# A decoder step: six counts of a sampled search placed behind the units of their pass, and new row blocks in the last norm

## The reference: what is computed

```python
h1 = LN1(alpha*x  + 0.5*SwiGLU_1(x))
h2 = LN2(alpha*h1 + W_out[attn_group(h1) | hgrn2_group(h1)])
y  = LN3(alpha*h2 + 0.5*SwiGLU_2(h2))
...
score = jnp.where(valid, score, -jnp.inf)   # sample tokens: 8192 cached keys and the new one
_, idx = lax.top_k(score, n_sel)            # n_sel = 256
...
xc = x32 - mu
var = jnp.mean(xc * xc, -1, keepdims=True)
return xc * lax.rsqrt(var + LN_EPS) * g + b
```

## Time and profile before

| what | value |
|---|---|
| median of 3 runs | 2416.02 us (2415.59 to 2416.42) |
| profiled execution | 2416.54 us, of which the span of the page is 2414.8 us |
| TensorE busy | 2340.9 us, 97% of the span |
| VectorE, GpSimd, ScalarE busy | 67%, 37%, 30% |
| mean granted clock of TensorE | 0.99 |

### The profile page before, as it was taken

The page is one execution under the profiler, slowest core; times in us unless marked ns, Lnnn a source line. Parts: engine busy times, 40 slices in busy tenths (PEclk is TensorE's granted clock), DMA queues, the critical chain, the costliest instruction groups (busy, mean ns, idle before and its releaser), DMA issues.

```text
span 2414.8 us, 33393 instructions
## 1 busy us (share of the span) xinstructions
PE 2340.9 (97%) x12317; PEld 1926.6 (80%) x12317; DVE 1612.7 (67%) x2577; ACT 714.9 (30%) x1441; POOL 886.7 (37%) x948
## 2 busy tenths in 40 slices
PE   8999999999999999999999899999999999999996
PEld 7888888888887556778777677888888888888885
DVE  6675666578975348897767844236575665678876
ACT  2122222210023246773332356314122222210014
POOL 5354444446475021110000133414244444445570
PEclk9999999999999999999999999999999999999998
DMA  6021222264411033330010112021012131256401
GB/s 184 18 96 53 88 71 70 100 256 148 144 58 35 1 93 114 105 101 20 2 28 2 41 40 69 4 71 35 27 61 80 62 105 53 73 206 243 144 18 71
DMA packets 138047, 192.58 MB, mean 80 GB/s; under 512 B 19112, under 2 KB 86264, under 8 KB 137632
## 3 DMA queue, kind: packets, MB, share of 16 engines
q1 hardware_dynamic: 130096, 169.97, 21.0%
q0 software_dynamic: 7792, 20.48, 3.0%
HBM read 160.10 MB, written 30.06 MB: 79 GB/s over the span
## 4 chain that ended last, share of the span: by engine, by line
PE 88%; DVE 7%; issue 2%; ACT 1%; POOL 1%; DMA 1%; SPq 0%; DVEq 0%; POOLq 0%; ACTq 0%
PE ps L2104 38%; PE ps L2198 16%; PE ps L794 9%; PE ps L799 7%; PE ps L1186 4%; PE ps L1074 2%; PE ps L2201 2%; PE ps L964 2%; PE ps L1048 2%; PE ps L850 1%; PE ps L875 1%; PE ps L1061 1%; PE ps L1014 1%; PE ps L885 1%; PE ps L897 1%
## 5 line engine op out<-in xcount | busy, mean ns | idle before, releaser
L2104 PE MATMUL ps<-big 128*128 128x258 f32 x1760 | 410.5, 381 | 5.1 <-DVE big L2517 4.6
L2104 PEld LDWEIGHTS ps<-big 128*128 128x128 f32 x1760 | 333.0, 190 | 57.1 <-issue 7.7
L2369 ACT ACTIVATE down_weights<-ps 128x258 f32<-128x258 f32 x370 | 142.8, 387 | 699.8 <-PE ps L2104 699.7
L2637 DVE TENSOR_TENSOR down_weights<-ps,down_weights 128x258 f32<-128x258 f32 x330 | 139.3, 425 | 261.5 <-ACT down_weights L2369 187.1
L794 PE MATMUL ps<-acts,weight_ring 128*128 128x344 f32 x768 | 236.9, 461 | 0.0
L794 PEld LDWEIGHTS ps<-acts,weight_ring 128*128 128x128 f32 x768 | 143.5, 192 | 74.6 <-issue 8.9
L2945 POOL TENSOR_TENSOR big<-weight_ring 128x256 f32<-128x256 f32 x100 | 75.6, 757 | 334.0 <-PE ps L2104 300.1
L2198 PE MATMUL ps<-big,aux 128*128 128x258 f32 x840 | 191.7, 382 | 4.0 <-DVE big L2750 4.0
L2198 PEld LDWEIGHTS ps<-big,aux 128*128 128x128 f32 x840 | 159.8, 191 | 29.6 <-DVE big L2750 5.6
L799 PE MATMUL ps<-weight_ring,acts 128*128 128x256 f32 (+3 forms) x720 | 176.3, 399 | 0.0
L799 PEld LDWEIGHTS ps<-weight_ring,acts 128*128 128x128 f32 (+1 forms) x720 | 126.2, 180 | 37.2 <-issue 9.3
(11 more groups left out here) (456 smaller groups left out, 4464.9 us busy)
## 6 DMA issues: line engine op xcount, KB each, us to landing
big<-scratch_hidden SPq DMA_DIRECT2D x12, 2838.0 KB, 11.0
weight_ring<-ffn_wd SPq DMA_DIRECT2D x8, 2816.0 KB, 9.8
scratch_hidden<-down_weights SPq DMA_DIRECT2D x40, 516.0 KB, 2.8
weight_ring<-ffn_wg SPq DMA_DIRECT2D x20, 1024.0 KB, 7.9
weight_ring<-ffn_wu SPq DMA_DIRECT2D x20, 1024.0 KB, 8.3
down_weights<-ffn_wd SPq DMA_DIRECT2D x4, 2816.0 KB, 20.2
weight_ring<-w_in SPq DMA_DIRECT2D x9, 1024.0 KB, 5.4
big<-x_prompt SPq DMA_DIRECT2D x8, 512.0 KB, 5.5
```

Source lines behind the costliest of these rows:

```text
L2104: last = M(PS[:, 3 * e + bank, 0:TQ], lhs[:, i, :], rhs[:, i, :], start=begin and i == 0, stop=end and i == n - 1, skip_group_check=True)
L2369: A(st(e, c), PS[:, 3 * e, 0:TQ], ACT.Copy).then_inc(cp_done, 1)
L2637: V.tensor_tensor(out, PS[:, 3 * e + bank, 0:TQ], st(e, part), ALU.add).then_inc(add_done, 1)
```

## The change

On TensorE, in the passes that `MASK_SLOTS` names, the count e = 1 moves behind all units of its pass. VectorE's program of this loop stays as it is. In the tail the five raw blocks are laid anew: the first, tokens 904 to 1031, holds the last 120 prompt tokens and the 8 sample tokens; the second begins at 776; the others at 512, 640 and 768 (8 tokens). The first two lie in the last quarter of the tokens. For these, part C of the last pair is cut in two: C2 (last quarter) is added ahead of part D, C1 after step 4. So both are complete before step 4, and they are turned behind its two halves; the fourth block of `turn_out` moves ahead of step 4. Blocks 3 and 4 (r = 3, 4) now wait until VectorE is done with r = 0 and 1, whose banks they take.

```diff
@@ the raw blocks @@
-        RAW0 = 4 * P
+        RAW_AT = (904, 776, 512, 640, 768)
         RAW_ROWS = (P, P, P, P, NB)
+        RAW_BANK = (0, 3, 6, 0, 3)
@@ TensorE, the loop of the recurrence @@
                     if len(here) > 1:
                         unit(here[0])
-                    if (t, lv, 1) in DEC_SLOTS:
+                    late = (t, lv) in MASK_SLOTS
+                    if (t, lv, 1) in DEC_SLOTS and not late:
                         count(DEC_SLOTS.index((t, lv, 1)))
                     for u in here[1:] if len(here) > 1 else here:
                         unit(u)
...
                     elif lv == 6:
                         for u in AFTER[t][1:3]:
                             unit(u)
+                    if late and (t, lv, 1) in DEC_SLOTS:
+                        count(DEC_SLOTS.index((t, lv, 1)))
@@ SyncE, the stores @@
-            for r in range(4):
+            for r in range(5):
                 sp.wait_ge(ln_done, 10 + r + 1)
-                sp.dma_start(O["y_prompt"][0, RAW0 + P * r:RAW0 + P * r + P, :], RAW_OUT[r]).then_inc(y_stored[r % 2], 16)
-            sp.wait_ge(ln_done, 15)
-            sp.dma_start(O["y_sample"][:, 0, :], RAW_OUT[4][0:NB]).then_inc(y_stored[0], 16)
+                rows = RAW_ROWS[r] if r else P - NB
+                sp.dma_start(O["y_prompt"][0, RAW_AT[r]:RAW_AT[r] + rows, :], RAW_OUT[r][0:rows]).then_inc(y_stored[r % 2], 16)
+                if r == 0:
+                    sp.dma_start(O["y_sample"][:, 0, :], RAW_OUT[0][P - NB:P]).then_inc(y_stored[0], 16)
@@ TensorE, the last pair and the turns @@
                     product(4, e, 2, down_w(o, 1, 1), down_h_sum(4), False, True, (down_w_rest(o, 1), down_h_rest(o, 0)))
+                    if ff and j == 6:
+                        turn_raw(e)
...
             def turn_raw(r):
-                pe.wait_ge(oc_done, outer_count(1, NP + 6, 1))
-                if r == 3:
+                if r < 2:
+                    pe.wait_ge(dir_done, direct_count(1, NP + 6, 1))
+                else:
+                    pe.wait_ge(oc_done, outer_count(1, NP + 6, 1))
+                if r == 2:
                     pe.wait_ge(y_copied, 8)
-                elif r == 4:
-                    pe.wait_ge(ln_done, 11)
+                elif r > 2:
+                    pe.wait_ge(ln_done, 11 + r - 3)
...
-                        elif ff and j == 6:
-                            turn_out((7, 5, 3, 4).index(k))
+                        elif ff and j == 6 and k in (7, 5, 3):
+                            turn_out((7, 5, 3).index(k))
+                            if k == 3:
+                                turn_out(3)
...
-            for r in range(5):
+            for r in range(2, 5):
                 turn_raw(r)
@@ VectorE, the additions of the last pair @@
-                if part == "A":
+                if part in ("A", "C2"):
                     link(last)
...
-                    down_outer_add(ff, j, e, "C")
+                    down_outer_add(ff, j, e, "C1" if ff and j == 6 else "C")
...
                 down_inner_add(ff, j, 1)
+                if ff and j == 6:
+                    for e in range(2):
+                        dve.wait_ge(add_done, add_count(ff, p, 1, e))
+                        down_outer_add(ff, j, e, "C2")
```

More of the change, by code:

```diff
@@ L222, in raw_rows @@
         def raw_rows(r):
-            return PS[0:RAW_ROWS[r], 2 * (r % 4):2 * (r % 4) + 2, :].rearrange("p u c -> p (u c)")
+            return PS[0:RAW_ROWS[r], RAW_BANK[r]:RAW_BANK[r] + 2, :].rearrange("p u c -> p (u c)")
         x_loaded = [sem(f"x_loaded{i}") for i in range(3)]
@@ L2057, in _ @@
                 store_block(b)
-            for r in range(4):
+            for r in range(5):
                 sp.wait_ge(ln_done, 10 + r + 1)
-                sp.dma_start(O["y_prompt"][0, RAW0 + P * r:RAW0 + P * r + P, :], RAW_OUT[r]).then_inc(y_stored[r % 2], 16)
-            sp.wait_ge(ln_done, 15)
-            sp.dma_start(O["y_sample"][:, 0, :], RAW_OUT[4][0:NB]).then_inc(y_stored[0], 16)
-            sp.wait_ge(y_stored[0], 16 * 5)
+                rows = RAW_ROWS[r] if r else P - NB
+                sp.dma_start(O["y_prompt"][0, RAW_AT[r]:RAW_AT[r] + rows, :], RAW_OUT[r][0:rows]).then_inc(y_stored[r % 2], 16)
+                if r == 0:
+                    sp.dma_start(O["y_sample"][:, 0, :], RAW_OUT[0][P - NB:P]).then_inc(y_stored[0], 16)
+            sp.wait_ge(y_stored[0], 16 * 6)
             sp.wait_ge(y_stored[1], 16 * 4)
@@ L2264, in turn_raw @@
             def turn_raw(r):
-                pe.wait_ge(oc_done, outer_count(1, NP + 6, 1))
-                if r == 3:
+                if r < 2:
[3 more added lines that the diff above has]
+                if r == 2:
                     pe.wait_ge(y_copied, 8)
-                elif r == 4:
-                    pe.wait_ge(ln_done, 11)
-                at = RAW0 + P * r
+                elif r > 2:
+                    pe.wait_ge(ln_done, 11 + r - 3)
+                at = RAW_AT[r]
                 for d in range(DT):
-                    last = T(PS[0:RAW_ROWS[r], 2 * (r % 4) + d // 4, P * (d % 4):P * (d % 4) + P],
+                    last = T(PS[0:RAW_ROWS[r], RAW_BANK[r] + d // 4, P * (d % 4):P * (d % 4) + P],
                              ACTS[:, d, at:at + RAW_ROWS[r]], IDENT[:, :])
@@ L2762, in down_outer_add @@
                 p, o = NP + j, DOWN_OUTER[j]
-                a, c0, n = {"A": (0, 0, 1), "D": (0, 1, 1), "C": (1, 0, 2)}[part]
-                src = {"A": st_down(e, 0), "D": PS[:, 3 * e, 0:TQ], "C": st_down(e, 1, 2)}[part]
+                a, c0, n = {"A": (0, 0, 1), "D": (0, 1, 1), "C": (1, 0, 2), "C1": (1, 0, 1), "C2": (1, 1, 1)}[part]
+                src = {"A": st_down(e, 0), "D": PS[:, 3 * e, 0:TQ], "C": st_down(e, 1, 2),
+                       "C1": st_down(e, 1), "C2": st_down(e, 2)}[part]
                 for di, tj in {1: [((0,), (0, 1)), ((1,), (0, 1))], 2: [((0,), (0,))], 7: [((1,), (0, 1))], 6: [((0,), (1,)), ((1,), (0, 1))],
```

## The result

| what | before | after |
|---|---|---|
| median of 20 runs of each, taken side by side | 2417.20 us (2410.05 to 2419.59) | 2420.82 us (2417.89 to 2423.10) |
| ratio of the times | | 1.0015, 95% interval 1.0008 to 1.0022 |
| profiled execution, its span | 2416.54, 2414.8 us | 2417.89, 2416.2 us |

The changed kernel is slower by 0.15%, which is within the 0.2% called no change, though the interval reaches a little over it; it leaves 1 out, so the loss is small but not nothing. The forecast of 2418.8 us was 2.8 above the runs of before then shown; the difference of the medians is 3.6. The profiled execution of after is the shortest of its 20.

A forecast was written before the change was run, and what follows sets the result against it. TensorE, busy for 97% of the span, was taken to bound the kernel. +5.0 - 0.3 - 1.9 = +2.8 us on the profiled 2416.54 gave 2419.3; the median, 0.5 lower, 2418.8 us, range 2413.5 to 2422.5.

The forecast's parts named there:

- idle of the four pairs, t = 1: In loop t = 1 TensorE idles 1.44 us between adjacent counts, at four places: 4 x 1.44 = 5.8 us.
- old wait and its dip, t = 1: In pass 5 of t = 1 the 2.14 us wait and the 2.82 us clock dip behind it go.
- tails product at the end of t = 1: VectorE's tails product starts only after the last compare, so the turn behind waits some 0.2 us more.
- falls behind the pairs: In t = 1 the new waits bring two falls of the clock at 2.0 us each: 4.0 us.
- loop t = 1: Counts moved in passes 3 to 6; all terms there, clock falls included, sum to +5.0 us.
- waits in t = 2: TensorE waits 2.5 us before the first count of pass 6, and a new 0.8 us before the turn.
- loop t = 2: Counts moved in passes 5 and 6: -3.58 + 2.5 + 0.8 = -0.3 us.
- last product of the tail: In the tail it ends 2.3 us later: 0.5 stall plus two turns of 0.87.
- tail: After the loops: 2.3 later product, 0.5 shorter additions, 3.7 less VectorE idle, together -1.9 us.
- rival C: At least three of four pairs in t = 1 lower the clock, at 2.82 us each: +7.3, 2423.3 us; 15%.
- Rival B: The new waits come in both loops but none lowers the clock: -3.2, 2412.8 us; 17%.
- rival D: The tail gives nothing: fourth block's turn stalls, last product ends 4 us later, +4.7, 2420.7 us; 10%.

The follow-up runs named there:

- experiment 2: Changed kernel with unread products of constants between paired counts: 11 (20 in t = 2) measured 2421.24 us; 5 (10 in t = 2) measured 2415.39 us.

## Why the prediction was right, and where it was not

| step | forecast | trace of after |
|---|---|---|
| idle of the four pairs, t = 1 | 4 x 1.44 = 5.8 | 4 x 1.37 = 5.5 |
| old wait and its dip, t = 1 | -2.14 - 2.82 | both gone |
| tails product at the end of t = 1 | +0.2 | 0 (the turn follows the level products without idle) |
| falls behind the pairs | 2 x 2.0 = 4.0 | 1.69 + 1.69 + 1.71 = 5.1 |
| loop t = 1 | +5.0 | 61.20 - 55.36 = +5.8 |
| waits in t = 2 | 2.5 and 0.8 | 2.52 and 0.64 |
| loop t = 2 | -0.3 | -0.9, -0.9 and +0.7 in three profiles |
| between the loops | not in the sum | -0.9, -0.9 and +1.1 |
| last product of the tail | 2.3 later | 20.59 - 18.30 = 2.3 later, from the start of the first turn to that of the turn behind the last product |
| tail | -1.9 | 34.40 - 36.29 = -1.9 |
| sum of the loops, the stretch between and the tail | +2.8 | 128.30 - 124.23 - 1.9 = +2.2, +2.2 and +5.7 in three profiles; +3.6 in the medians |

**The waits were right,** to within 0.2 us each, because VectorE's round could be read from one place in the trace of before and moved.

**The falls were sized wrongly twice, and the two errors cancel only in part.** The step "I take two falls at the cheaper price" was off: there were three in every profile of after, at 1.7 us instead of 2.0, so 5.1 us and not 4.0. Three was the condition of rival C, but its price of 2.82 us was far too high: with the measured price its sum would be +1.0 + 5.1 - 0.3 - 1.9 = +3.9, beside +2.8 in the forecast and 3.6 in the medians. The prices came from falls behind waits of 2.14 and 3.58 us, where the low clock lasted about twice as long. A window inside the first fall of after, and one inside that of before in t = 1:

```profile
1200.80:1204.10 3.30, 3.30 (x8) 2.67 (x9) 3.16 (x8) 0.00 (x0) 0.00 (x0) 0.50 0.02 5
```

```profile
1211.30:1217.90 6.60, 6.09 (x16) 2.31 (x17) 6.32 (x13) 2.23 (x4) 0.00 (x0) 0.50 0.00 0
```

In both the low level reaches less than 0.2 us further to either side. In before it began while TensorE still waited for the count (1211.81). So the reason given for the cheaper price, that part of a slow stretch would lie in the waits, is true of the falls in before; in the pairs of t = 1 none of it did, and the price was lower because the stretch was shorter.

**That the sum is so near is in part luck.** The loop t = 1 came out 0.8 us dearer than forecast. In two of the three profiles the loop t = 2 was 0.6 and the stretch between the loops 0.9 us cheaper than forecast, in the third both were about 1 us dearer.

**Two figures of the prediction do not fit.** Rival B's 2412.8 us lies below the range 2413.5 to 2422.5, which is said to hold most of it. A last product 4 us later, as in rival D, makes the sum +4.5, not +4.7.

**Rival B fell.** The clock did not stay up: gaps of 1.37 us beside 64-row products were enough at three of the four places, and experiment 2 shows that filling them is enough to keep it up. The Trainium skill (TensorE: Matmul & The Clock Gate, section Why this matters for your kernels) warns there only of gaps longer than these; the trace does not agree, and the measured falls, 5.1 us in t = 1, decide. The 3.2 us of idle at a granted 1.00, which spoke for B, stand in another stage and inside the idle, where after too reads 1.00; they did not show what a gap beside the level products does.

**Rival D fell:** the stall ahead of the fourth turn was 0.34 us in its first half and 0.5 in all, as worked out.

**A term was missing.** In before a fall lies between the loops, at 1245.6; the second half of the products of pass 0 (line 974) takes 2.03 us there and 1.16 in after, 0.87 us less. In two of three profiles of after the fall is gone, in the third two stand there. The prediction used that row as a bound and not as a cost that the change could shift.

## What to carry to other kernels

Price a wait of TensorE together with the fall of the clock that can follow it, read from the unit behind the wait against its like elsewhere; here the falls cost as much as the idle (5.1 and 5.5 us). When two steps are bound by a round trip to another engine, do not put them next to each other: something that needs neither belongs between them. Five small products whose result nobody reads kept the clock up and saved 5.4 us, but left the round itself uncovered; level products, which had to be done anyway, covered most of it too and saved 11.8. To remove a wait, move work to its place rather than the waiting instruction to the next of its kind.

## What the runs showed of the hardware

A stretch with a busy TensorE can run in part at the lower clock because of idle time before it: from 1200.68 the granted clock was 0.68 over 5.32 us with TensorE busy all the time, and 1.00 in the level products directly ahead; with the idle filled it was 1.00 throughout. Identical waits are followed by a fall in one execution of a kernel and by none in another (with the late counts in t = 2 alone, 2.14 us of idle in t = 1, then 6.34 and 6.44 us in two executions and 3.62 us in a third for the same unit). A float32 product of 128 x 128 by 128 columns shows as two records, and five of them took 1.36 us back to back.
